# Attention rows set by a tile's number of keys, and eight rows of gathers alone, in a streaming encoder with gathered experts

## The chip, the core and the metric

The kernel runs on one core of a Trainium2 chip. The metric is the device time of one execution in microseconds (us), lower being better; a version is judged by the median of its runs.

## The reference

One layer of an encoder over 1024 prompt tokens and 128 sample tokens (eight requests of 16), each a vector of 1024 float32 values. What matters of it, shortened:

```python
a = rmsnorm(h)
qd, kd, vd, qs, ks, vs = split(a @ w_in)              # 8 heads of 64 each
w = softmax(qd1 @ kd1) - lam * softmax(qd2 @ kd2)     # differential attention, chunk-causal
diff = rmsnorm(w @ vd)
z = qs @ ks / 8                                       # stick-breaking attention, causal
wts = exp(log_sigmoid(z) + sum_of_later(log_sigmoid(-z)))
h += concat(diff, wts @ vs) @ w_out
# experts: per token 8 heads x 16 chosen of 16384
c = rmsnorm(h)
q = (c @ w_query).reshape(t, 8, 2, 128)
s1, i1 = top_k(q[:, :, 0] @ sub_keys[0].T, 16); s2, i2 = top_k(q[:, :, 1] @ sub_keys[1].T, 16)
top, sel = top_k(s1[..., None] + s2[..., None, :], 16)
idx = expert numbers of sel;  g = softmax(top)
coef = g * gelu(einsum('td,thkd->thk', c, expert_u[idx]))
h += einsum('thk,thkd->td', coef, expert_v[idx])
h += (p @ w_ple) * sigmoid(rmsnorm(h) @ w_pgate)
y = rmsnorm(h)
```

## The kernel before

Tokens are worked in nine tiles of 128 (`T = 9`; eight of the prompt, `TP = 8`, and one of the samples). Every token picks 128 experts, so a tile has 128 **rows** (`ROWS`): row r of a tile gathers, for each of the 128 tokens, one vector of `expert_u` and one of `expert_v`, 128 x 1024 floats each. There are 1152 rows in all, and the program is laid out along them. A **position** e is the 128 rows of tile e.

For one row: POOL issues the gather of u into a ring of four buffers (`gather_u`, L585) and, 16 rows later, the gather of v into a ring of eight (`gather_v`, L602). DVE takes the dot product of the u row with the tile's tokens (`dot`, L1498). After 16 rows ACT applies gelu (L1146) and DVE makes the coefficients (L1527). Of the v rows DVE adds some, those that the table `vector_rows` names (in the first 64 rows of a position four of 16, and five of 16 in positions 5 and 6), to `acc` (`add_row`, L1512). For the rest ACT spreads the coefficient onto a diagonal (`spread`, L1158, a ring of four) and PE multiplies with it into `sum_ps` (`add_rows`, L779). A gather waits until its buffer has been used: u on the dot four rows back, v on the sum eight rows back.

While the rows of tile e go through, the engines prepare tile e + 1, in two stages. **Attention** has four steps m = 0 to 3 (`attending_step`), each of two differential and two stick-breaking heads. In a step PE makes six score tiles in turn in two halves of `z_ps` (`attention_scores`, L810 and L812, j = 0 to 5). DVE takes the maximum of the first four (`maximum`, L1658), and ACT exponentiates each once its maximum is there (`softmax_top`, L1241). PE may overwrite a half only when that is done. Then come DVE's `subtract_half` (L1664 to L1669), ACT's `log_term` (L1249 to L1251), DVE's `break_stick` (L1677 to L1684), ACT's `raise_stick` (L1271), the transposes of the weights on PE (`turn_weights`, L825) with ACT's copies (L1258), and the products with the values (`weigh_values`, L837). For tile e + 1 a score tile has 128 x (e + 2) columns. **Routing** follows: `square_heads` and `norm_heads` on DVE with a power on POOL between them (`power`, L576), `turn_heads`, `project_heads` on PE (L722), `square_tokens` (L1559), then the queries, the key scores and the search for the best 16 on DVE, up to the new list of experts (L1645) and the gates.

The order of each engine is written out by hand. `go(end)` issues an engine's part of the rows up to `end`, and what follows it in the code stands behind those rows in that engine's queue. All engines are in order, so an operation that waits holds the rows behind it. Where things stand is given by two functions, `attend_at(e, m, k)` and `route_at(e, k)`: k counts 16 places in a step and 64 in the routing. In positions 1 to 6 the steps take rows 0 to 63 and the routing rows 64 to 127. Position 0 packs the four steps into rows 92 to 107 (the input projection runs before, L676), position 7 has the samples' attention in rows 0 to 79, and position 8 the end of the network (L1918 on). Before row 0 there are steps and a routing with no gathers beside them (e = -1). SP loads keys and values for a step when the former step no longer needs them (`load_keys`, `load_values`).

## Time and profile before

| | us |
|---|---|
| three runs | 4246.7, 4250.4, 4270.1 |
| median | 4250.4 |
| the profiled execution, its own time | 4267.0 |
| its span, first to last instruction | 4265.2 |
| PE busy | 3316.2 (78%) |
| DVE busy | 2908.0 (68%) |
| POOL busy | 2747.3 (64%) |
| ACT busy | 1164.7 (27%) |

The execution that was profiled is 16.6 us above the median of the three. Busy time of PE is modelled, since its matmuls overlap; the busy time of POOL is the issuing of gathers. An average over the span says little here, since positions have different limits: a position is read by the time between the dot of its first row and that of the next position's first row, and by what DVE and POOL wait for in it. Positions 1 to 6 lie between 881.6 and 3331.8 us of the span.

### The profile page before, as it was taken

The page shows a single profiled execution, that of the slowest core. Times are in us where ns is not written, and L with a number is a line of the kernel's source. Part 1 is how long each engine was busy: PE and PEld are TensorE (multiplying, and loading weights), DVE is VectorE, ACT ScalarE, POOL GpSimd, SP SyncE. Part 2 cuts the span into 40 slices and gives each one's busy share as a digit, 9 for nine tenths or more (in the row PEclk, how much of TensorE's full clock was granted, in tenths as well). Part 3 has the DMA queues.
Part 4 walks back from the last instruction along what each step waited for, and adds up shares of the span by engine and source line. Part 5 has one row for each costly group of instructions (what it writes and reads, how often), then busy time and mean ns, then how long its engine had stood idle before and what let it go on. Part 6 is the DMA issues. An engine that isn't in the chain of part 4 may idle for free.

```text
span 4265.2 us, 32462 instructions
## 1 busy us (share of the span) xinstructions
PE 3316.2 (78%) x9380; PEld 1593.9 (37%) x9380; DVE 2908.0 (68%) x5551; ACT 1164.7 (27%) x2256; POOL 2747.3 (64%) x2355
## 2 busy tenths in 40 slices
PE   7788976767968786887778778877887687758777
PEld 3334434333424433443344334433443343323333
DVE  2176754577687678768776877687768667686775
ACT  2211115134114312421342134313531233111111
POOL 0016653367777777777777776777677656567784
PEclk9899987988999999999899988999899998879998
DMA  5238987489999999999999999999999999899996
GB/s 197 92 135 319 344 335 248 157 302 372 342 354 380 370 329 358 379 345 357 350 324 335 340 343 334 330 351 353 340 335 366 338 327 357 313 336 370 378 373 234
DMA packets 452607, 1369.22 MB, mean 321 GB/s; under 512 B 47696, under 2 KB 118224, under 8 KB 451408
## 3 DMA queue, kind: packets, MB, share of 16 engines
q0 software_dynamic: 331776, 1208.11, 76.6%
q1 hardware_dynamic: 95312, 135.96, 9.2%
q10 hardware_dynamic: 25344, 23.07, 1.6%
q8 instruction: 79, 1.29, 0.1%
q14 instruction: 96, 0.79, 0.1%
HBM read 1338.65 MB, written 28.31 MB: 320 GB/s over the span
## 4 chain that ended last, share of the span: by engine, by line
PE 39%; POOL 21%; issue 13%; DVE 11%; DMA 10%; ACT 5%; another core or an unknown queue 1%; ACTq 0%; SPq 0%; POOLq 0%; DVEq 0%
PE sum_ps L779 14%; POOL v_ring L602 10%; POOL u_ring L585 10%; PE z_ps L722 7%; PE z_ps L676 6%; DMA u_ring<-expert_u_in,idx_tile 4%; DMA v_ring<-expert_v_in,idx_tile 4%; DVE u_ring L1498 3%; PE sum_ps L676 2%; PE z_ps L810 2%; DVE arena L1589 1%; PE out_ps L837 1%; DVE neg_max L1658 1%; PE z_ps L976 1%; PE group_ps L825 1%
## 5 line engine op out<-in xcount | busy, mean ns | idle before, releaser
L779 PE MATMUL sum_ps<-v_ring,diag 128*128 128x512 f32 x3172 | 1694.9, 671 | 631.8 <-DMA v_ring<-expert_v_in,idx_tile 342.9
L585 POOL DMA_INDIRECT u_ring<-expert_u_in,idx_tile x1152 | 1363.1, 1183 | 766.3 <-DVE dots L1498 417.3
L1498 DVE CUSTOM_DVE_ANT_0 u_ring<-u_ring,c_rows 128x1024 f32<-128x1024 f32 x1152 | 1404.6, 1225 | 598.3 <-DMA u_ring<-expert_u_in,idx_tile 535.4
L602 POOL DMA_INDIRECT v_ring<-expert_v_in,idx_tile x1152 | 1331.2, 1156 | 360.2 <-issue 327.9
L779 PEld LDWEIGHTS sum_ps<-v_ring,diag 128*128 128x128 f32 x3172 | 618.4, 210 | 1443.4 <-issue 894.7
L1512 DVE SCALAR_TENSOR_TENSOR acc<-v_ring,coef,acc 128x1024 f32<-128x1024 f32 x350 | 450.4, 1287 | 9.0 <-DMA v_ring<-expert_v_in,idx_tile 9.0
L1158 ACT ACTIVATE diag<-ident,coef 128x128 f32<-128x128 f32 x793 | 287.2, 394 | 517.1 <-PE sum_ps L779 369.2
L722 PE MATMUL z_ps<-weights,arena 128*128 128x512 f32 x768 | 343.2, 600 | 3.4 <-ACT arena L1120 3.4
L1658 DVE TENSOR_REDUCE neg_max<-z_ps 128x1 f32<-128x128 f32 (+7 forms) x128 | 96.5, 755 | 262.3 <-PE z_ps L812 231.7
L676 PE MATMUL z_ps<-weights,arena 128*128 128x512 f32 x576 | 257.9, 604 | 21.1 <-issue 12.3
L722 PEld LDWEIGHTS z_ps<-weights,arena 128*128 128x128 f32 x768 | 146.8, 193 | 182.9 <-issue 176.1
L1241 ACT ACTIVATE arena<-z_ps,neg_max 128x128 f32<-128x128 f32 (+7 forms) x128 | 94.7, 740 | 437.9 <-DVE neg_max L1658 347.8
L837 PEld LDWEIGHTS out_ps<-arena 128*128 128x128 f32 x1152 | 163.4, 210 | 103.1 <-issue 87.4
L810 PE MATMUL z_ps<-arena,qd 128*128 128x512 f32 (+3 forms) x384 | 149.6, 499 | 46.7 <-DMA qd<-qk_turned 40.6
L837 PE MATMUL out_ps<-arena 128*128 128x64 f32 x1152 | 158.2, 287 | 32.4 <-ACT arena L1258 25.7
L825 PE MATMUL group_ps<-ident,arena 128*128 128x128 f32 x576 | 104.2, 292 | 98.9 <-ACT arena L1258 86.6
L676 PEld LDWEIGHTS z_ps<-weights,arena 128*128 128x128 f32 x576 | 109.3, 193 | 155.7 <-issue 143.4
L676 PE MATMUL sum_ps<-weights,v_ring 128*128 128x512 f32 x288 | 141.7, 648 | 15.0 <-ACT v_ring L1187 6.3
L1258 ACT COPY arena<-group_ps 128x512 f32<-128x512 f32 (+3 forms) x192 | 90.6, 472 | 193.0 <-PE group_ps L825 147.1
L1146 ACT ACTIVATE gelus<-dots 128x16 f32<-128x16 f32 x72 | 15.4, 214 | 443.7 <-DVE dots L1498 294.6
L1589 DVE FIND_INDEX8 arena<-arena 128x8 uint32<-128x128 f32 (+1 forms) x432 | 134.4, 329 | 0.0
L608 POOL TENSOR_TENSOR p_stat<-p_stat,minus_half 128x1 f32<-128x1 f32 x9 | 9.6, 1061 | 193.2 <-DVE p_stat L1734 193.2
(189 smaller groups left out, 3106.4 us busy)
## 6 DMA issues: line engine op xcount, KB each, us to landing
u_ring<-expert_u_in,idx_tile POOLq DMA_INDIRECT x1152
v_ring<-expert_v_in,idx_tile POOLq DMA_INDIRECT x1152
weights<-w_in_in SPq DMA_DIRECT2D x6, 2048.0 KB, 18.6
u_ring<-w_query_in SPq DMA_DIRECT2D x16, 512.0 KB, 5.2
weights<-w_out_in SPq DMA_DIRECT2D x2, 4096.0 KB
weights<-w_query_in SPq DMA_DIRECT2D x1, 8192.0 KB, 39.4
qk_turned<-arena ACTq DMA_DIRECT2D x24, 256.0 KB, 4.5
arena<-x_all_in SPq DMA_DIRECT2D x9, 512.0 KB
```

Source lines behind the costliest of these rows:

```text
L585: pool.indirect_dma_start(u_rows[r % U_RING][:, :], None, ins["expert_u"], bass.IndirectOffsetOnAxis(ap=idx_tile[:, e % 2, at:at + 1], axis=0)
L602: pool.indirect_dma_start(v_rows[g % V_RING][:, :], None, ins["expert_v"], bass.IndirectOffsetOnAxis(ap=idx_tile[:, e % 2, at:at + 1], axis=0)
L676: mm = nc.tensor.matmul(bank, home.aT[:, k, :], w_in[:, k, g * W:(g + 1) * W], start=(k == 0), stop=(k == KC - 1))
L722: mm = nc.tensor.matmul(acc_ps[:, bank, :], inT[:, k, :], weights[:, k, half * W:(half + 1) * W], start=(k == 0), stop=(k == KC - 1))
L779: mm = nc.tensor.matmul(sum_ps[:, half * W:(half + 1) * W], diag[:, by_tensor[g] % DIAGS, :], v_rows[g % V_RING][:, half * W:(half + 1) * ...
L810: nc.tensor.matmul(z_ps[:, j % 2, a:a + w], q, kt.rearrange("p j k -> p (j k)")[:, a:a + w], start=True, stop=a + w < width)
L825: mm = nc.tensor.transpose(group_ps[:, (k - a) * P:(k - a + 1) * P], src[:, k * P:(k + 1) * P], const.ident)
L837: mm = nc.tensor.matmul(out_ps[:, 64 * h:64 * h + 64], wT[:, k * P:(k + 1) * P], v[:, k, 64 * (h % 2):64 * (h % 2) + 64], start=(k == 0), ...
L1158: nc.scalar.mul(diag[:, j % DIAGS, :], const.ident, coef[:, (step - 1) % 2, g % TOP:g % TOP + 1]).then_inc(diag_done, 1)
L1498: nc.vector.tensor_tensor_reduce(row, row, c_rows[e % 2][:, :], 1.0, 0.0, ALU.mult, ALU.add, dots[:, s % 2, r % TOP:r % TOP + 1]).then_inc ...
L1512: nc.vector.scalar_tensor_tensor(acc[:, :], row, weight, acc[:, :], ALU.mult, ALU.add).then_inc(v_added, 1)
L1589: last = nc.vector.max_index(found[:, m, 8 * half:8 * half + 8], vals[:, m, 8 * half:8 * half + 8], src[:, m, :])
```

## The change

Positions 1 to 6 get another table of rows. Rows 0 to 7 have neither attention nor routing (`LATER = 8`). The four steps then share 5e + 32 rows: 37 in position 1, 42, 47, 52, 57, and 62 in position 6, so that a step has 9.25 rows in position 1 and 15.5 in position 6, where it had 16 in each. The routing has what is left: 83 rows in position 1, then 78, 73, 68, 63, and 58 in position 6, where it had 64. Positions -1, 0, 7 and 8 keep their tables.

Beside this, some operations get another place k. On ACT each `softmax_top` now stands at the k of the maximum that it waits for (2, 3, 5, 6) instead of in pairs at 0 and 4. PE's scores j = 4 move from 4 to 5. In the routing `square_heads` moves from 2 to 4, `norm_heads` and PE's `turn_heads` from 4 to 5, `project_heads` 0 from 5 to 6, and POOL's first power from behind the gather of row 2 + 3 to behind that of 4 + 2. These moves hold in all positions.

```diff
+LATER = 8
+        def attention_rows(e):
+            return 5 * e + 32
         def attend_at(e, m, k):
-            return FREE_ROWS + 4 * m + k // 4 if e == 0 else ROWS * e + TOP * m + k
+            if e < 0:
+                return ROWS * e + TOP * m + k
+            if e == 0:
+                return FREE_ROWS + 4 * m + k // 4
+            return ROWS * e + LATER + (TOP * m + k) * attention_rows(e) // 64
         def route_at(e, k):
...
-            return ROWS * e + 64 + k
+            if e < 0:
+                return ROWS * e + 64 + k
+            return ROWS * e + LATER + attention_rows(e) + (ROWS - LATER - attention_rows(e)) * k // 64
...
-                go(route_at(e, 2) + U_RING)
+                go(route_at(e, 4) + U_RING - 1)
                 power(e + 1, 0)
...
-                go(attend_at(e, m, 4))
+                go(attend_at(e, m, 5))
                 attention_scores(i, 4, n)
...
-                go(attend_at(e, m, 0))
+                go(attend_at(e, m, 2))
                 softmax_top(i, 0, m, n)
+                go(attend_at(e, m, 3))
                 softmax_top(i, 1, m, n)
                 go(attend_at(e, m, 4))
                 if m:
                     take_out(e, m - 1)
+                go(attend_at(e, m, 5))
                 softmax_top(i, 2, m, n)
+                go(attend_at(e, m, 6))
                 softmax_top(i, 3, m, n)
...
-                go(route_at(e, 2))
+                go(route_at(e, 4))
                 square_heads(t)
-                go(route_at(e, 4))
+                go(route_at(e, 5))
                 norm_heads(t)
```

PE's `turn_heads` goes from `route_at(e, 4)` to `route_at(e, 5)` and `project_heads(t, 0)` from 5 to 6 in the same way.

**ACT, position 4, second step (m = 1), from its first exponential to the first `log_term`.** `diag` is the spread coefficient of a v row, `neg_max` the maximum that DVE makes. Before:

```order
L1241 ACT_TABLE_LOAD
L1241 ACTIVATE arena,total<-z_ps,neg_max 128x768 x2
L1158 ACTIVATE diag<-ident,coef 128x128 x4
L1265 COPY mix<-out_ps 128x2x128
L1241 ACTIVATE arena,total<-z_ps,neg_max 128x768 x2
L1158 ACTIVATE diag<-ident,coef 128x128 x3
L1249 ACTIVATE arena<-z_ps 128x768
```

After:

```order
L1252 ACTIVATE arena,total<-z_ps,neg_max 128x768
L1169 ACTIVATE diag<-ident,coef 128x128
L1252 ACTIVATE arena,total<-z_ps,neg_max 128x768
L1276 COPY mix<-out_ps 128x2x128
L1169 ACTIVATE diag<-ident,coef 128x128
L1252 ACTIVATE arena,total<-z_ps,neg_max 128x768 x2
L1260 ACTIVATE arena<-z_ps 128x768
```

Seven spread rows stood between the first exponential and the logarithm, and none between the first two exponentials; now two stand there, one of them between the first two.

**DVE, the same step, from its first maximum to the first `subtract_half`.** Before:

```order
L1658 TENSOR_REDUCE neg_max<-z_ps 128x1
L1498 ISA u_ring,dots<-u_ring,c_rows 128x1024
L1498 ISA dots 128x1
L1658 TENSOR_REDUCE neg_max<-z_ps 128x1
L1498 ISA u_ring,dots<-u_ring,c_rows 128x1024
L1498 ISA dots 128x1
L1498 ISA u_ring,dots<-u_ring,c_rows 128x1024
L1498 ISA dots 128x1
L1658 TENSOR_REDUCE neg_max<-z_ps 128x1
L1498 ISA u_ring,dots<-u_ring,c_rows 128x1024
L1498 ISA dots 128x1
L1658 TENSOR_REDUCE neg_max<-z_ps 128x1
```

After:

```order
L1672 TENSOR_REDUCE neg_max<-z_ps 128x1
L1512 ISA u_ring,dots<-u_ring,c_rows 128x1024
L1512 ISA dots 128x1
L1672 TENSOR_REDUCE neg_max<-z_ps 128x1
L1512 ISA u_ring,dots<-u_ring,c_rows 128x1024
L1512 ISA dots 128x1
L1512 ISA u_ring,dots<-u_ring,c_rows 128x1024
L1512 ISA dots 128x1
L1523 TENSOR_SCALAR acc<-v_ring,coef 128x1024
L1672 TENSOR_REDUCE neg_max<-z_ps 128x1 x2
```

The dot that stood between the third and the fourth maximum is gone from there; of the 16 rows of the step 13 are left.

## Rows read from the trace of the kernel before

**Rows 1.** From the page: the share of the DMA engines in 40 slices, in tenths.

```profile
DMA  5238987489999999999999999999999999899996
```

**Rows 2.** Windows: length; PE, PEld, DVE, ACT, POOL busy; clock; DMA share; GB/s.

```profile
881.60:1070.80 189.20, 137.30 (x410) 71.93 (x411) 132.32 (x214) 78.62 (x156) 146.46 (x129) 0.86 0.99 375
1070.80:1272.20 201.40, 162.55 (x392) 69.44 (x391) 149.45 (x362) 33.38 (x79) 154.98 (x132) 0.94 0.94 347
1272.20:1461.80 189.60, 147.11 (x462) 76.47 (x460) 139.13 (x214) 84.46 (x155) 145.41 (x128) 0.90 0.99 373
1461.80:1664.00 202.20, 162.08 (x395) 69.10 (x394) 149.31 (x362) 34.26 (x80) 152.42 (x133) 0.94 0.94 347
1664.00:1858.40 194.40, 154.79 (x568) 85.68 (x567) 147.00 (x215) 95.50 (x174) 152.96 (x127) 0.94 0.99 369
1858.40:2060.80 202.40, 159.40 (x387) 68.11 (x386) 149.25 (x361) 32.98 (x77) 156.15 (x133) 0.95 0.95 347
2060.80:2276.40 215.60, 169.53 (x611) 95.64 (x611) 154.13 (x214) 101.64 (x173) 155.68 (x125) 0.89 0.93 335
2276.40:2487.30 210.90, 164.46 (x394) 70.32 (x394) 149.09 (x362) 33.38 (x78) 156.37 (x133) 0.93 0.92 336
2487.30:2709.50 222.20, 179.96 (x636) 103.08 (x635) 166.03 (x217) 106.73 (x168) 157.29 (x128) 0.88 0.92 330
2709.50:2910.20 200.70, 157.37 (x400) 68.35 (x399) 149.24 (x362) 34.07 (x79) 154.42 (x133) 0.97 0.96 352
2910.20:3129.60 219.40, 182.12 (x667) 102.43 (x666) 172.78 (x218) 111.69 (x166) 153.03 (x127) 0.90 0.94 341
3129.60:3331.80 202.20, 162.10 (x423) 70.98 (x423) 151.16 (x368) 34.47 (x82) 154.66 (x130) 0.97 0.98 359
```

**Rows 3.** Waits in position 4's attention, 2060.8 to 2276.4: total, times, longest.

```profile
ACT arena L1241 <- DVE neg_max L1658: 63.6, 14, 9.2
...
DVE neg_max L1658 <- PE z_ps L812: 28.7, 6, 7.5
...
POOL u_ring L585 <- DVE dots L1498: 24.6, 9, 5.2
```

**Rows 4.** Waits in position 1's attention, 881.6 to 1070.8.

```profile
DVE u_ring L1498 <- DMA u_ring<-expert_u_in,idx_tile: 45.3, 38, 3.0
PE sum_ps L779 <- ACT diag L1158: 34.0, 7, 20.6
```

**Rows 5.** Timeline of one step's start in position 4: start, us, what, idle before.

```profile
2181.64 6.57 PE L779 MATMUL sum_ps<-v_ring,diag 128*128 128x512 f32 x8 [6.44 <-issue]
...
2189.76 0.96 DVE L1658 TENSOR_REDUCE neg_max<-z_ps 128x1 f32<-128x768 f32 x1 [6.09 <-PE z_ps L812]
...
2192.12 0.94 POOL L585 DMA_INDIRECT u_ring<-expert_u_in,idx_tile  x1 [5.06 <-DVE dots L1498]
...
2194.30 3.60 PE L779 MATMUL sum_ps<-v_ring,diag 128*128 128x512 f32 x8
```

**Rows 6.** Windows of position 0's four steps, four rows and 256 keys each.

```profile
660.80:683.20 22.40, 14.79 (x53) 10.58 (x53) 15.73 (x29) 14.75 (x28) 10.70 (x8) 0.67 0.65 208
683.20:703.50 20.30, 16.22 (x65) 10.14 (x64) 11.30 (x25) 13.35 (x29) 7.62 (x8) 0.92 0.70 234
703.50:724.80 21.30, 17.45 (x67) 10.97 (x66) 11.26 (x25) 13.32 (x29) 7.63 (x8) 0.84 0.72 237
724.80:744.00 19.20, 15.27 (x60) 9.34 (x58) 11.19 (x24) 13.49 (x30) 7.61 (x8) 0.91 0.64 203
```

**Rows 7.** Lines by shape, position 4's attention: count, busy, mean ns, idle before.

```profile
L1498 DVE CUSTOM_DVE_ANT_0 u_ring<-u_ring,c_rows 128x1024 f32<-128x1024 f32 x64 | 77.4, 1222 | 26.8 <-DMA u_ring<-expert_u_in,idx_tile 26.2 <-issue 0.4
...
L1512 DVE SCALAR_TENSOR_TENSOR acc<-v_ring,coef,acc 128x1024 f32<-128x1024 f32 x16 | 20.7, 1294 | 0.0
```

**Rows 8.** Waits in the first 32 routing rows of position 1, 1070.8 to 1174.3.

```profile
DVE mix L1559 <- PE z_ps L722: 5.8, 1, 5.8
...
POOL rstat L576 <- DVE rstat L1564: 5.1, 1, 5.1
```

More of the change, by code:

```diff
@@ L1013, in _ @@
                 t = e + 1
-                go(route_at(e, 4))
+                go(route_at(e, 5))
                 turn_heads(t)
-                go(route_at(e, 5))
+                go(route_at(e, 6))
                 project_heads(t, 0)
@@ L1855, in _ @@
                 go(route_at(e, 1))
-                go(route_at(e, 2))
+                go(route_at(e, 4))
                 square_heads(t)
-                go(route_at(e, 4))
+                go(route_at(e, 5))
                 norm_heads(t)
```

## The prediction

> **What bounds the kernel now.** I first read the share of the DMA engines along the span [rows 1]: it stands at nine tenths in almost every slice from the tenth on. So for most of the time the gathers themselves are the bound, and a change of order can only win what is missing to a full share. The page's slices are too coarse to say where that is, so I cut positions 1 to 6 into their attention and routing halves of 64 rows [rows 2]; the two halves of a position are two neighbouring rows there. Three things are to be seen. In positions 1 to 3 the attention halves take 189.2, 189.6 and 194.4 us at a share of 0.99: 2.96 us a row, and nothing to win. In positions 4 to 6 they take 215.6, 222.2 and 219.4 us at 0.92 to 0.94. The routing halves take 200.7 to 210.9 us at 0.92 to 0.98. Multiplying each length by what its share lacks of one gives 2 + 12 + 2 + 12 + 2 + 12 + 15 + 17 + 18 + 8 + 13 + 4 = 117 us. That is about all that this change can gain.
>
> Then I asked who makes the late attention halves slow. In position 4 POOL stands still for 24.6 us before u gathers, in nine waits, until a dot has freed a buffer, and DVE stands for 28.7 us in six waits for PE's score tiles; ACT waits 63.6 us for maxima [rows 3]. The timeline of one step links them [rows 5]. ACT has taken up its first pair of exponentials, which wait for DVE's maxima two and three rows further on, so it spreads no coefficients, and PE is idle for 6.44 us. When it goes on, its eight matmuls of v rows take 6.57 us, where eight of the same kind take 3.60 us a little later. Only behind them come the scores for the third maximum. DVE waits 6.09 us for these, no dot is done, and POOL waits 5.06 us. The ring of four u buffers is then used up and the DMA engines run out of work. In position 1 the same ACT block exists (PE waits 34.0 us for the diagonals), but PE has little to do there, and DVE's own idle time is nearly all for u rows, 45.3 us [rows 4]; so it costs nothing.
>
> **The price of a row and of a step.** The profiled execution took 4267.0 us, 16.6 us more than the median of 4250.4 us; I work out a difference in the former and take it off the latter. A row that nothing else delays costs 2.95 us, from position 1's attention (189.2 / 64 [rows 2]); I use it for rows alone too. On DVE one row costs 1.22 us for the dot (77.4 / 64) and 1.29 us for each added v row, 16 of them in 64 rows [rows 7], so 1.54 us. For positions 5 and 6 I count 5 in 16, as the table of added rows has it, so 1.62 us.
>
> A step costs the larger of two things: its rows at 2.95 us, or DVE's own work plus w, the time that DVE waits in it for its partners. DVE's work per step is the busy time of the attention half less the rows that leave it, over four: position 1 (132.3 - 27 x 1.54) / 4 = 22.7 us, then 26.3, 30.2, 33.9, position 5 (166.0 - 7 x 1.62) / 4 = 38.7, and 42.4 us [rows 2]. The rows at 2.95 us are 27.3, 31.0, 34.7, 38.4, 42.0 and 45.7 us. So the new table puts the steps close to DVE's own work everywhere, and w decides.
>
> **What w will be.** No row shows it for the new steps. From below: in position 1's attention DVE is idle for 189.2 - 132.3 = 56.9 us, 45.3 of them for u rows [rows 2, 4], which leaves 2.9 us a step at 16 rows. From above: position 0 packs a step of 256 keys into four rows, and DVE is idle there for 6.7, 9.0, 10.0 and 8.0 us, 8.4 us on average [rows 6], with nearly no rows to fill the waits. By row count between these two, steps of 9 to 12 rows have about 5.5 us: I take that for positions 1 to 3. In position 4 it is now (215.6 - 154.1 - 26.2) / 4 = 8.8 us [rows 2, 7], and the block described above is most of it. With each exponential at the place of its maximum, ACT can spread before it and PE is not starved before the third score tile. But the first maximum of a step now comes one row after the scores were asked for instead of two, and the third and fourth stand together. I take 7 us for positions 4 to 6, between 5.5 and 8.8.
>
> **Attention, the sum.** Eight rows alone are 23.6 us, and four steps follow. Position 1: 23.6 + 4 x 28.2 = 136.4, against 45 rows now at 2.96 = 133.0: +3. Position 2: 150.8 against 50 rows, 148.1: +3. Position 3: 23.6 + 4 x 35.7 = 166.4 against 167.1: -1. Position 4: 23.6 + 4 x 40.9 = 187.2 against 60 rows at 3.37, 202.1: -15. Position 5: 206.4 against 222.2 and one routing row, 225.3: -19. Position 6: 23.6 + 4 x 49.4 = 221.2 against 219.4 and six routing rows, 238.4: -17. Together -46 us. With w = 2.9 everywhere all steps fall to their rows' price and the sum is -96; with w = 8.4 everywhere it is +6.
>
> **Routing, the sum.** The routing half of position 1 is 201.4 - 64 x 2.95 = 12.6 us over its rows. Its first 32 rows take 1174.3 - 1070.8 = 103.5 us, 9.1 over 32 x 2.95, and in them DVE waits 5.8 us for PE's product before `square_tokens`, and POOL 5.1 us for the second power [rows 8]. The distance from `norm_heads` to `square_tokens` was 6 rows (k 4 to 10) and is 6 again in position 1 (row 51 to 57), so I keep the 9.1 us; in positions 4 to 6 it is 5 rows. What goes with 83 rows is the crowding of the searches, 3 or 4 us. So position 1: 83 x 2.95 + 9.1 = 254.0 against 19 attention rows and 201.4, 257.6: -4. In the same way positions 2 and 3 give -4 and -5, position 4 (68 rows, its surplus kept) -2, position 5 (63 rows) 0, position 6 (58 rows, surplus of 13.4 us in fewer rows) +3. Together -12 us; between 0, if all the surplus is in fixed waits, and -30, if half of it goes.
>
> **The smaller edits.** POOL's first power now stands one gather earlier while the squares stand where they did relative to it or later, so POOL holds u row 4 + 3 until a dot, the squares and the power are done. Free at best, and at worst once the 5.1 us of a power's wait [rows 8] in each of six positions; I take +1 us each, +6, since three u rows are in flight then. Position 7's squares come two rows later, which gives the samples' rows more time to land; position 0's, one row. I cost these at nothing: neither is at a place where DVE is ahead. The keys of a step are reloaded once its fourth score tile is read, and have 7 rows of time in position 1 where they had 13; at 2.95 us that is 21 us, for 192 KB at 375 GB/s. It stays hidden.
>
> **The forecast:** -46 - 12 + 6 = -52 us. 4267.0 becomes 4215, and the median 4250 becomes **4198 us**.
>
> **Rivals.** First, **the DMA engines fill up**: w falls to what position 1 shows, and the routing loses half its surplus. The sum is -96 - 30 + 6 = -120, capped by the 117 us above: 4133 us. For it speaks that positions 1 to 3 hold 0.99 in attention; against it, that DVE's work in the late steps is within 4 us of the rows' price.
>
> Second, **the gain is given back in the early positions**. They have 0.99 now and can only lose. If a step of 9 to 12 rows waits as long as one of four, w = 8.4 us, positions 1 to 3 lose 15 + 14 + 11 us, and 4 to 6 gain only 9 + 13 + 12: +6 - 12 + 6 = 0, so 4250 us. For it: the wait for a step's own chain (scores, maximum, exponential, logarithm, scan, exponential, transpose, product) does not shrink with the rows. Against it: those waits are hidden by dots and added rows, of which there are twice as many or more.
>
> Third, **slower, by PE's clock**. The granted clock is 0.86 to 0.90 in five attention halves of six [rows 2], that is a part of the time at the lower of its two levels, and the two groups of eight matmuls, 6.57 us after an idle stretch of 6.44 us and 3.60 us in full work [rows 5], show the two levels, 1.2 and 2.4 GHz. The change adds eight rows of little PE work before each attention, and in the routing of positions 1 to 4 spreads the work thinner. If each step starts at the lower level, its scores, and again its last transposes and products, take twice as long on the path of w. I put that at 5 us a step, from the 3 us by which the slow group exceeds the fast one, once at the start and less at the end. Over 24 steps it is +120, so +68 in all: 4318 us. It decides from 3 us a step on. Against it: ACT's block, which now makes PE idle, goes. The Trainium skill, in "TensorE: Matmul & The Clock Gate", Part 1 on the clock gate, says that the throttled state is the default and that activity releases it, which speaks for this rival; by that rule alone sparse rows before each attention bring the time to this rival's 4318 us, and by the granted clock of 0.94 to 0.97 in the routing halves, themselves sparse in PE work, to none of it.
>
> That the change does nothing is no rival: the orders differ in every step.
>
> **How the numbers follow.** The forecast has 0.50, the first rival 0.12, the second 0.21, the third 0.17. What a measurement of this kernel can tell from no change is about 0.5%, 21 us. Faster by more than that are the first rival and nearly all of the forecast's spread, and a little of the second: 0.64. Within it: 0.19. Slower: 0.17. The range takes in w from 2.9 us, -96 - 12 + 6 = -102, 4148 us and somewhat below, and above the second rival with 25 us of the way to the third: 4140 to 4275 us. The forecast's own range is 4160 to 4232 us.
>
> **What would show it.** In the profile of the changed kernel: the DMA share of positions 4 to 6 up to 0.95 or more over their attention rows, with POOL's wait for dots there down from 24.6 us to some 12; ACT's wait for maxima halved and PE's wait for diagonals in position 1 well under 34.0 us; position 1 as long as now within 5 us and positions 5 and 6 shorter by 15 to 20 us each. If w is wrong, the early positions show it: at 8.4 us position 1 is over 10 us longer and its attention share under 0.95. If the clock is the cause, the granted clock of the attention rows falls below 0.8. It would also be wrong if the eight rows alone cost more than 2.95 us each, or if the routing's surplus grew in positions 5 and 6 by more than the 3 us counted.

## The result, and the profile after

| | before | after |
|---|---|---|
| runs, us | 4246.7, 4250.4, 4251.1, 4270.1 | 4309.0, 4319.9, 4324.7, 4328.4 |
| median | 4250.7 | 4322.3 |
| ratio, 95% interval | | 1.0124 [1.0087, 1.0161] |
| profiled execution, and its span | 4267.0, 4265.2 | 4328.4, 4326.6 |
| positions 1 to 6 in it | 2450.2 | 2504.8 |

The changed kernel is slower, where I had forecast 4198 us: by 1.2% by the ratio on record, by 1.7% by the two medians. Why the two differ is not shown. A ratio of 1.0124 belongs to a kernel before of 4269 us, and beside the first experiments below it did run at 4268.8 us. The fourth run of the kernel before, 4251.1 us, is new here. In the profiled executions positions 1 to 6 lose 54.6 us, position 7 loses 9, position 8 loses 3, and position 0 gains 6.

The page of the changed kernel looks almost like the one of before: the busy times of the engines, and the share of the DMA engines in tenths, to be held against [rows 1].

```profile
PE 3371.6 (78%) x9380; PEld 1616.6 (37%) x9380; DVE 2905.5 (67%) x5551; ACT 1159.6 (27%) x2249; POOL 2731.4 (63%) x2355
...
DMA  5348997489999999999999999899899889899996
```

Only five eights in the slices 26 to 35, where there was one, tell that something was lost. Cut into stages it is plain. These are windows of the changed kernel (length; PE, PEld, DVE, ACT, POOL busy; granted clock; DMA share; GB/s): the four steps of positions 1 and 2, which answer to the attention rows in [rows 2] but hold 37 and 42 rows and not 64, and the four steps of positions 3, 4 and 6 with 47, 52 and 62 rows.

```profile
900.40:1020.10 119.70, 95.47 (x330) 54.38 (x329) 89.91 (x152) 65.60 (x126) 84.53 (x74) 0.87 0.94 353
1299.40:1438.60 139.20, 111.55 (x401) 62.12 (x399) 104.52 (x163) 78.91 (x137) 97.78 (x83) 0.90 0.93 344
1700.90:1868.50 167.60, 138.34 (x486) 80.36 (x485) 119.26 (x174) 85.98 (x150) 112.64 (x93) 0.83 0.91 326
2119.20:2304.50 185.30, 151.22 (x553) 88.02 (x553) 135.40 (x187) 95.68 (x159) 130.13 (x103) 0.89 0.91 323
2964.90:3185.50 220.60, 178.76 (x673) 102.17 (x672) 169.18 (x211) 109.64 (x164) 154.48 (x122) 0.91 0.90 326
```

Before, the share was 0.99 in positions 1 to 3 and 0.92 to 0.94 in the later ones [rows 2]. Now it is 0.90 to 0.94 in all of them: the early positions have lost their full share, and the late ones have gained none to speak of. A row of the steps costs 3.24 us in position 1 (119.7 / 37) and 3.57 us in position 3. By stage, in us (first dot to first dot, one profiled execution):

| position | 8 rows alone | four steps | routing | sum | before |
|---|---|---|---|---|---|
| 1 | 24.1 | 119.7 | 258.3 | 402.1 | 390.6 |
| 2 | 21.0 | 139.2 | 241.9 | 402.1 | 391.8 |
| 3 | 20.3 | 167.6 | 230.0 | 418.0 | 396.8 |
| 4 | 20.6 | 185.3 | 214.7 | 420.7 | 426.5 |
| 5 | 20.6 | 197.0 | 206.8 | 424.3 | 422.9 |
| 6 | 21.4 | 220.6 | 195.5 | 437.5 | 421.6 |

Next, who waits. These are waits of the changed kernel in position 4's steps, in the form of [rows 3] (waiter and line, what it waits for; total, times, longest in us; L1252 is the exponential, L1672 the maximum, L596 the gather of u, L1512 the dot; `remote` is a release that the profile ties to no instruction).

```profile
ACT arena L1252 <- DVE neg_max L1672: 47.4, 12, 23.7
...
POOL u_ring L596 <- DVE dots L1512: 26.8, 9, 6.4
...
DVE neg_max L1672 <- PE z_ps L823: 24.3, 5, 9.9
...
DVE neg_max L1672 <- remote: 8.3, 1, 8.3
```

POOL still waits 26.8 us for dots, and DVE some 33 us for score tiles, now in fewer and longer waits. The place has changed. I added up DVE's idle time before each maximum of a step, over the 24 steps of positions 1 to 6: before the third maximum it was about 96 us and is now 3, as forecast; before the fourth it was 4 and is now 14; but before the **first** it was about 41 us and is now 132. A timeline (start, us, what, idle before) of the start of position 3's third step shows what a first maximum waits for.

```profile
1793.75 1.33 PE L848 MATMUL out_ps<-arena 128*128 128x64 f32 x10 [0.35 <-ACT arena L1269]
...
1794.92 1.30 PE L821 MATMUL z_ps<-arena,qd 128*128 128x512 f32 x4
...
1796.05 0.39 PE L823 MATMUL z_ps<-chunk_mask,ident 128*128 128x128 f32 x2
...
1796.48 0.82 DVE L1672 TENSOR_REDUCE neg_max<-z_ps 128x1 f32<-128x640 f32 x1 [7.11 <-PE z_ps L823]
...
1798.71 0.95 POOL L596 DMA_INDIRECT u_ring<-expert_u_in,idx_tile  x1 [3.47 <-DVE dots L1512]
```

The scores of a new step stand on PE behind the products with the values of the step before, and these wait for ACT's copies of the transposed weights. That tail (scan, exponential, transposes, copies, products) takes its time whatever the number of rows. With 16 rows in a step it was mostly over when DVE came to the first maximum; with the 11 or 12 here it is not: DVE stands for 7.11 us, and POOL for 3.47 us after it.

Two more waits are to be seen in position 6's steps. L1523 is DVE's first addition of a position, which overwrites `acc` and so needs the former tile's output to be stored; L1541 makes the coefficients after a gelu.

```profile
POOL u_ring L596 <- DVE dots L1512: 29.9, 6, 12.0
...
DVE acc L1523 <- DMA summed<-acc: 13.3, 1, 13.3
...
DVE coef L1541 <- ACT gelus L1157: 11.4, 2, 6.4
```

### The profile page after: what moved, and what is told of

Its sections match the earlier page's. It is cut to its first block, busy times and chain, and to the rows that moved or that the text cites. A ratio compares the mean times of both kernels' runs of the same rounds, so it can differ in the third digit from the quotient of the medians.

```text
span 4326.6 us, 32452 instructions
## 1 busy us (share of the span) xinstructions
PE 3371.6 (78%) x9380; PEld 1616.6 (37%) x9380; DVE 2905.5 (67%) x5551; ACT 1159.6 (27%) x2249; POOL 2731.4 (63%) x2355
## 3 DMA queue, kind: packets, MB, share of 16 engines
q0 software_dynamic: 331776, 1208.11, 75.6%
## 4 chain that ended last, share of the span: by engine, by line
PE 27%; POOL 18%; issue 13%; DVE 12%; DMA 9%; ACT 6%; another core or an unknown queue 1%; SPq 0%; ACTq 0%; DVEq 0%; POOLq 0%
PE sum_ps L790 12%; POOL u_ring L596 9%; POOL v_ring L613 9%; PE z_ps L733 6%; DMA v_ring<-expert_v_in,idx_tile 4%; DMA u_ring<-expert_u_in,idx_tile 4%; DVE u_ring L1512 3%; PE z_ps L821 2%; PE out_ps L848 2%; DVE arena L1603 2%; PE group_ps L836 1%; DVE acc L1526 1%; ACT arena L1269 1%; PE z_ps L687 1%
## 5 line engine op out<-in xcount | busy, mean ns | idle before, releaser
L790 PE MATMUL sum_ps<-v_ring,diag 128*128 128x512 f32 x3172 | 1716.8, 679 | 564.2 <-DMA v_ring<-expert_v_in,idx_tile 344.8
L596 POOL DMA_INDIRECT u_ring<-expert_u_in,idx_tile x1152 | 1341.3, 1164 | 840.4 <-DVE dots L1512 498.9
L1512 DVE CUSTOM_DVE_ANT_0 u_ring<-u_ring,c_rows 128x1024 f32<-128x1024 f32 x1152 | 1402.5, 1225 | 582.0 <-DMA u_ring<-expert_u_in,idx_tile 506.9
L790 PEld LDWEIGHTS sum_ps<-v_ring,diag 128*128 128x128 f32 x3172 | 628.6, 213 | 1404.5 <-issue 843.1
L1672 DVE TENSOR_REDUCE neg_max<-z_ps 128x1 f32<-128x128 f32 (+7 forms) x128 | 96.1, 755 | 272.1 <-PE z_ps L823 238.1
L1252 ACT ACTIVATE arena<-z_ps,neg_max 128x128 f32<-128x128 f32 (+7 forms) x128 | 94.6, 740 | 370.4 <-DVE neg_max L1672 310.0
L836 PEld LDWEIGHTS group_ps<-ident,arena 128*128 128x128 f32 x576 | 75.8, 159 | 160.9 <-ACT arena L1269 119.4
```

Of the source, the lines that this page charges most:

```text
L596: pool.indirect_dma_start(u_rows[r % U_RING][:, :], None, ins["expert_u"], bass.IndirectOffsetOnAxis(ap=idx_tile[:, e % 2, at:at + 1], axis=0)
L790: mm = nc.tensor.matmul(sum_ps[:, half * W:(half + 1) * W], diag[:, by_tensor[g] % DIAGS, :], v_rows[g % V_RING][:, half * W:(half + 1) * ...
L836: mm = nc.tensor.transpose(group_ps[:, (k - a) * P:(k - a + 1) * P], src[:, k * P:(k + 1) * P], const.ident)
L1512: nc.vector.tensor_tensor_reduce(row, row, c_rows[e % 2][:, :], 1.0, 0.0, ALU.mult, ALU.add, dots[:, s % 2, r % TOP:r % TOP + 1]).then_inc ...
```

## The experiments

Ten kernels ran, in three groups. Each group had the kernel before beside it on its own chip, where its median was 4268.8, 4278.2 and 4298.9 us, so ratios to it are compared, not times. The first group has the two orders alone, the eight rows alone and the store first on the changed kernel; the third has the two kernels with later maxima; the second has the rest. None of them leaves out work. Stage times are from one profiled execution each, of positions 1 to 6. The runs of one kernel lie 9 to 45 us apart, so a difference of a few us between two kernels' stages means nothing by itself.

### The order of attention alone

```diff
-                go(attend_at(e, m, 0))
+                go(attend_at(e, m, 2))
                 softmax_top(i, 0, m, n)
+                go(attend_at(e, m, 3))
                 softmax_top(i, 1, m, n)
...
-                go(attend_at(e, m, 4))
+                go(attend_at(e, m, 5))
                 attention_scores(i, 4, n)
```

with exponentials 2 and 3 at 5 and 6, on the table of before.

> The kernel before with one part of the change alone: the exponentials of ACT at the places of their maxima and PE's fifth score tile one place later; all tables of rows as before. Theory (the loss comes from the denser steps, the order itself helps): DVE's wait for the third maximum, 4 to 7.5 us in each step of positions 4 to 6, goes, and the time falls by 30 to 45 us, to 4206 to 4220 us. Rival (the order moves the wait to the next step's first maximum): 4250 us within 10, with first waits of 7 us or more. Rival (the order is what makes the changed kernel slow): over 4270 us.

Measured: 4221.9 us, ratio 0.9895 [0.9875, 0.9915], some 45 us, as expected. This is the fastest of all, and faster than both kernels of the case. Its positions 1 to 6 take 2399.6 us, 50.6 less than before. Windows of its attention, 64 rows each, in positions 1, 4, 5 and 6:

```profile
876.70:1064.90 188.20, 139.83 (x394) 72.49 (x395) 131.85 (x215) 77.58 (x151) 143.89 (x130) 0.83 1.00 382
2061.60:2259.30 197.70, 163.73 (x612) 92.60 (x611) 155.06 (x215) 103.64 (x174) 157.63 (x127) 0.95 0.99 367
2463.00:2662.50 199.50, 171.02 (x641) 99.55 (x640) 166.59 (x218) 109.41 (x170) 159.12 (x126) 0.91 0.98 367
2865.60:3068.80 203.20, 174.63 (x668) 99.64 (x667) 173.22 (x217) 113.48 (x167) 150.92 (x126) 0.94 0.99 365
```

The late ones took 215.6, 222.2 and 219.4 us at 0.92 to 0.94 [rows 2]; they are now at 0.98 and 0.99. And its waits in position 4, against [rows 3]:

```profile
ACT arena L1241 <- DVE neg_max L1661: 26.5, 11, 5.7
...
DVE neg_max L1661 <- PE z_ps L812: 1.8, 2, 1.1
...
POOL u_ring L585 <- DVE dots L1501: 1.7, 1, 1.7
```

ACT's wait for maxima fell from 63.6 to 26.5 us, DVE's for scores from 28.7 to 1.8, and POOL's for dots from 24.6 to 1.7. So the part of the change that puts an exponential at the place of its maximum is worth 1% by itself, and what is left of the change, the table of rows, costs 2.3% beside it (1.0124 over 0.9895 is 1.023; with the two medians of the case it would be 2.8%), if the two add up.

### The order of routing alone

`square_heads` at 4, `norm_heads` and `turn_heads` at 5, `project_heads` 0 at 6, and POOL's first power one gather earlier, all as in the change, on the table and the attention order of before.

> The kernel before with the moves of the routing alone (squares and norm of the heads, the turn, the first projection, POOL's first power). Theory: within 8 us of before, 4243 to 4259 us. Rival (these moves hold POOL's gathers back in every position, 5 us each): 4280 us.

Measured: 4271.6 us, 1.001 [0.9991, 1.0029]; positions 1 to 6 take 2445.0 us against 2450.2. These moves do nothing that can be measured, and the rival's 5 us in every position is excluded. The 6 us in all that I had put on the power lie inside the interval, so they are neither shown nor refuted.

### Eight rows alone, but 64 rows of attention

```diff
         def attention_rows(e):
-            return 5 * e + 32
+            return 64
```

on the changed kernel. Steps have 16 rows again; the routing is left with 56.

> The changed kernel with 64 rows of attention in each of positions 1 to 6, behind the eight rows alone; the routing has 56 rows. Theory (the density of the steps is the cause): the first maximum of a step waits under 3 us in positions 1 to 3, these are each 10 to 15 us shorter than in the changed kernel in their attention, and the time is 4235 to 4265 us, with some 20 us lost in the routing by 56 rows. Rival (the eight rows and the sum's change in the middle of a step are the cause): the second step is still the slow one, 55 us or more, and the time stays at 4300 us or above.

Measured: 4366.4 us, 1.0221 [1.0193, 1.0249]; positions 1 to 6 take 2550.5 us. That thin steps are the only cause is refuted: with full steps the kernel got slower still, though in part by a wait that was small in the changed kernel. Its second step of a position takes 53 to 66 us. Asked what DVE's first addition (L1523, nine times) waits for, its trace answers:

```profile
L1523 DVE TENSOR_SCALAR acc<-v_ring,coef x9: 746/752/754, 336.6 to 3991.0; 128x1024 f32<-128x1024 f32 x9
...
  DMA summed<-acc: 90.3, 6
```

15 us in each of six positions. SP stores the tile's output behind the values of the second step, which it loads only when the former step's products have read the old ones. With the table moved by eight rows this comes later than the addition that needs the store. I had walked past this queue in the prediction.

### The store ahead of the values

```diff
                 for m in range(4):
                     load_keys(i, m)
-                    load_values(i, m)
                     if i >= 2 and m == 1:
                         store(i - 2)
+                    load_values(i, m)
```

Done once on the changed kernel:

> The changed kernel with SP's store of the finished sum ahead of the values of the second step instead of behind them. Theory: DVE's wait of 13.3 us for the store in position 6 and of 1.8 us in position 5 goes, and the time falls by 8 to 15 us, to 4307 to 4314 us. Rival (the wait is only taken over by the next one of the same step): 4322 us within 5.

Measured: 4306.8 us, 1.0078 [1.0053, 1.0103], and no wait for the store is left, where the changed kernel had 15.1 us in two waits. Positions 1 to 6 take 2490.1 us, 14.7 less than the changed kernel. The two intervals overlap, though, and of the 14.7 us position 3, which had no such wait, has 11.3 and position 6 has 6.7: that the store costs this much in the changed kernel is likely, not shown. And once on the kernel with 64 rows behind eight:

> The run e4 (eight rows alone, then steps of 16 rows) with SP's store of the finished sum ahead of the values of the second step. Theory (DVE waits 13 to 15 us in each of the six positions for that store, and most of it is lost time): 55 to 80 us below e4, 4286 to 4311 us, with rows 24 to 39 of a position at 52 us or less. Rival (the wait is cover for others): within 20 us of e4, 4345 us or above.

Measured: 4324.8 us, 1.0118 [1.0074, 1.0161]: a gain of 1.0% on the run above, some 44 us where 55 to 80 were expected, with intervals that don't overlap; positions 1 to 6 take 2509.1 us. Windows of position 4, steps and routing:

```profile
2121.90:2332.70 210.80, 164.00 (x610) 93.65 (x608) 154.38 (x214) 98.34 (x168) 157.37 (x126) 0.91 0.94 343
...
2332.70:2523.30 190.60, 151.46 (x368) 66.88 (x369) 137.01 (x342) 31.01 (x73) 138.02 (x117) 0.92 0.91 328
```

By the ratios the store is 0.5% of the change's loss. Without it the two tables, thin steps with long routing and full steps with short routing, are 0.4% apart, which the intervals don't separate, and both are some 2% behind the order of before with its exponentials moved. So with full steps, and without the late store, eight rows alone in front still cost 2.2% (1.0118 over 0.9895), about as much as the whole table of the change.

Two things make up this cost, read against the kernel with the attention order alone. The eight rows take only 20 to 24 us, 2.7 us a row, but the 56 rows of routing behind them still take 191.9 us on average, where 64 took 204.5: a row taken out of the routing gives back 1.6 us, not 2.95. And the steps, 16 rows each in both kernels, take 1230.0 us in the six positions against 1172.3, so 57.7 us more (in position 4, 210.8 against 197.7). Nothing was made thinner there; the steps only stand elsewhere among the rows. DVE's idle time before it makes coefficients is 50.9 us in these steps and was 3.7. The coefficients of 16 rows fall due where a step used to begin, and that is now its middle. Position 4's main wait of this kind:

```profile
DVE coef L1541 <- ACT gelus L1157: 9.0, 3, 5.5
```

### Fewer rows for attention, none alone

The best kernel so far, the one with the attention order alone, with another split in two sizes (it has the changed kernel's functions for the places):

```diff
+LATER = 0
+        def attention_rows(e):
+            return 56
```

> The run e1 (the kernel before with the attention's order alone) with attention in rows 0 to 55 of positions 1 to 6, 14 rows a step, and routing in 72 rows; no rows alone. Theory (a step is bound by its own chain, so a row taken out of it saves about 1.7 us and costs 2.95 us or more in the routing): 20 to 50 us above e1, 4242 to 4272 us, most of it in positions 4 to 6. Rival (density costs nothing, the shift does): within 10 us of e1, 4212 to 4232 us.

Measured: 4259.8 us, 0.9962 [0.9935, 0.999], which is 0.7% over the kernel with 64 rows. Its steps are 88 us shorter in the six positions for 48 rows fewer, 1.8 us a row, and its routing is 134 us longer for 48 rows more, 2.8 us a row. Position 4, steps and routing:

```profile
2069.00:2250.50 181.50, 149.66 (x578) 87.31 (x577) 142.00 (x197) 99.38 (x164) 143.61 (x111) 0.94 0.97 353
...
2250.50:2481.30 230.80, 176.45 (x425) 74.27 (x424) 161.28 (x379) 36.29 (x86) 172.33 (x150) 0.93 0.93 343
```

Then `return 48`, with `LATER = 2`, 12 rows a step:

> As e8, with two rows alone and then 12 rows a step, attention in rows 2 to 49. Theory: waits of 6 to 10 us for the first maximum of the steps in positions 4 to 6, a step there no shorter than 45 us, position 1 unchanged within 6 us; 80 to 170 us above e1, 4300 to 4390 us. Rival (density costs nothing): 4240 us or less.

Measured: 4318.2 us, 1.0126 [1.0059, 1.0193], 2.3% over the 64 rows and as slow as the changed kernel. Its steps in positions 1, 4 and 6:

```profile
891.60:1032.50 140.90, 114.23 (x379) 61.75 (x377) 106.87 (x178) 72.59 (x141) 109.21 (x97) 0.90 1.01 381
...
2083.90:2256.90 173.00, 140.42 (x552) 83.24 (x551) 129.21 (x178) 92.99 (x154) 125.23 (x95) 0.94 0.91 323
...
2938.10:3136.70 198.60, 163.34 (x628) 96.86 (x627) 147.55 (x178) 105.59 (x152) 122.15 (x96) 0.89 0.84 299
```

48 rows at 3.60 us in position 4 and at 4.14 us in position 6, where 64 rows cost 3.09 and 3.18 us each. Thin steps lose, and the more so the fewer rows they have, as expected; DVE's idle time before first maxima goes from 29 us with 64 rows to 94 with 56 and 165 with 48. Here no step is shifted by eight rows, and the store is not late; with 56 rows DVE has no idle time before coefficients in the steps either, so there the loss is the thinning alone (with 48 rows that idle time is 17.6 us). Two expectations for 48 rows were missed: five of the twelve steps in positions 4 to 6 took 38 to 42 us where none under 45 was expected, and position 1 is 6.9 us shorter than with 64 rows, not unchanged within 6.

### Sixteen rows alone

With eight rows alone the coefficients of 16 rows fall due in the middle of a step, and DVE waits for ACT's gelu there; with 16 they would again fall due at its start. So `LATER = 16`, 64 rows of attention, 48 of routing, the store first, and the routing order of before.

> The run e1 with the steps shifted by 16 rows, attention in rows 16 to 79 and routing in 48, the store of the sum first as in e7. The steps stand to the groups of 16 rows as in the kernel before, but the sum changes inside the first. Theory (a shift by half a group puts gelu and the coefficients into the middle of a step's chain): the four steps take 3 to 10 us less per position than in e7, and DVE's waits for gelu under 1 us each. The routing in 48 rows takes 180 us or more against 203 us for 64 rows in e1, so the total is 4350 to 4420 us. Rival (the routing's time goes with its rows): 4260 us or less.

Measured: 4420.7 us, 1.0325 [1.0274, 1.0375]. DVE's waits for gelus fell from 51 us to 4 in the attention rows, but the four steps came out at 214.5 us a position and not below the 205.0 of the eight-row kernel: the store is late again (it still stands behind the keys of the second step), 75.6 us before L1523 in six waits, and the first steps are 56 to 72 us long. Without their first step they are 2.9 us shorter. The expectation was missed, and how much the moved gelus cost by themselves stays open. The routing behind shows again what squeezing it brings; position 4:

```profile
2424.80:2602.00 177.20, 138.53 (x340) 61.97 (x339) 125.16 (x324) 26.80 (x63) 117.33 (x101) 0.90 0.85 305
```

177.2 us for 48 rows, at a share of 0.85. On average it is 177.7 us, somewhat under the 180 expected, and again 1.7 us back for each row taken out of 64. I read this as a chain that the stage has of its own; no run here takes that chain apart.

### Later maxima

If a first maximum only stands too early in a short step, it should help to move it. Scores 2 to 5 on PE, the four maxima on DVE and the four exponentials on ACT go to places 4 to 7, and the first subtraction, logarithm and transposes to 8. On the changed kernel with its store first:

```diff
-                go(attend_at(e, m, 2))
+                go(attend_at(e, m, 4))
                 maximum(i, 0, n)
-                go(attend_at(e, m, 3))
+                go(attend_at(e, m, 5))
                 maximum(i, 1, n)
```

> The run e6 (the changed kernel, store of the sum first) with the four maxima of a step, their exponentials and the score tiles behind them at places 4 to 7 instead of 2, 3, 5 and 6, and the first subtraction at 8, so that three or four rows stand ahead of a step's first maximum instead of one or two. Theory (a dense step is bound by the length of its chain, and where DVE waits in it does not matter): the wait for the first maximum falls by half or more, later waits grow, and the time is within 0.4% of e6, 1.004 to 1.012 of before. Rival (the loss is the place of the first maximum, one row behind the scores): 0.6% or more below e6, at or under 1.002 of before.

Measured: 4378.7 us, 1.0197 [1.0151, 1.0243], 1.2% over the same kernel without the move. On the best kernel, with 16 rows a step:

> The same move of the maxima on the run e1, with 16 rows a step. Theory: e1 waits 52 us in all for maxima in positions 1 to 6, 26 of them for first ones; with three rows ahead these go, and the time is 0 to 15 us below e1, 0.986 to 0.9895 of before. Rival (the chain behind the maxima then has too few rows, and the wait moves there): 0.992 or above.

Measured: 4286.9 us, 0.9971 [0.9948, 0.9994], 0.8% slower than it. The group of all maxima on the page (x128; busy, mean ns; idle before them and its main releaser), first of the changed kernel, then of the one with later maxima:

```profile
L1672 DVE TENSOR_REDUCE neg_max<-z_ps 128x1 f32<-128x128 f32 (+7 forms) x128 | 96.1, 755 | 272.1 <-PE z_ps L823 238.1
```

```profile
L1671 DVE TENSOR_REDUCE neg_max<-z_ps 128x1 f32<-128x128 f32 (+7 forms) x128 | 96.7, 757 | 290.8 <-PE z_ps L823 216.8
```

and of the kernel with the attention order alone:

```profile
L1661 DVE TENSOR_REDUCE neg_max<-z_ps 128x1 f32<-128x128 f32 (+7 forms) x128 | 96.3, 754 | 172.0 <-PE z_ps L812 153.8
```

Putting the maxima later doesn't take the wait away, 290.8 against 272.1 us (275.8 with the store first); it moves it. Over the 24 steps of positions 1 to 6, and against the same kernel without the move, the wait before first maxima fell from 134 to 75 us and the one before third maxima rose from 5 to 59. I read this as the chain of a step starting later and so ending later. The sum of these waits grew by 7 us only, while positions 1 to 6 took 45.1 us more (with 16 rows a step, 38.0 us more), so most of the loss is not in them. Some 17 us of each may be the third group's chip, where the kernel before is 0.7% slower. And part of both ratios lies outside these steps: in position 0, where a step has four rows and the move reaches it too, the four steps of the kernel with 16 rows took 144.0 us instead of 84.0, and the whole position 606.7 us instead of 580.8. What is refuted is that a later first maximum helps; what remains is the length of the chain against the length of the step.

## Why the prediction was wrong, point by point

**Where the loss is.** Positions 1 to 6 of the profiled executions, each line from the positions' sums, with us a position in the last column:

| from, to | us | where it lies |
|---|---|---|
| before, attention order alone | -50.6 | -8.4: ACT's block ahead of the third maximum |
| attention order, changed kernel with store first | +90.5 | +15.1: rows alone +21.1; steps -25.8 for 14.5 rows fewer; routing +19.7 for 6.5 rows more |
| store first, changed kernel | +14.7 | +2.4: in part DVE behind the late store, 15.1 us in two waits |
| sum | +54.6 | 2450.2 to 2504.8 |

In the second line a row taken out of the steps gives back 1.8 us, and one put into the routing costs 3.0 us. Rows alone are cheap, 2.6 us, but the eight that stand there were taken out of the steps at 1.8. These are differences of single executions.

**The bound and the first diagnosis** were right. ACT's early exponentials held PE, PE the third score tile, and that the u ring; undoing only this won 50.6 us in positions 1 to 6 of the 117 us that the shares lacked. I had put -46 us on the whole of attention; the order of attention alone, without the table, brings -58 us in the attention rows.

**The term that failed is w, DVE's wait in a step.** The forecast took 5.5 us in positions 1 to 3 and 7 us in 4 to 6. Worked out from the trace after by the same formula (a step's mean length less DVE's work per step) it is 7.2, 8.5, 11.7, 12.4, 10.5 and 12.8 us, 10.5 on average. The step that failed is the choice of bounds: I read w at 16 rows from position 1 and at four rows from position 0, found 2.9 and 8.4, and took these for the ends. Both are of short tiles, with 384 and 256 keys. The chain of a step grows with the keys, to 1024 in position 6, and its tail reaches into the next step, so 8.4 us was no upper bound. The kernel with 48 rows shows the growth at one row count: with 12 rows in each step DVE is idle for 8.5, 8.2, 11.4, 11.0, 11.1 and 12.8 us a step in positions 1 to 6.

The trace of before had a warning. The prediction worked w out for position 4 alone, 8.8 us. By the same sum position 5 has (222.2 - 166.0 - 15.0) / 4 = 10.3 us, over the supposed upper end at 16 rows a step. Its 15.0 us are the wait for u rows:

```profile
DVE u_ring L1498 <- DMA u_ring<-expert_u_in,idx_tile: 15.0, 11, 3.1
```

Two limits of this reading. The 2.9 and 8.8 us leave out the wait for u rows, and the 10.5 holds it; without it the changed kernel's w is 5.8, 7.5, 11.7, 11.2, 7.5 and 10.0 us, 9.0 on average, so in position 1 the forecast was good and in position 5 nearly. And w isn't the chain alone: steps of 16 rows became 2.4 us longer by standing behind eight rows (57.7 us over 24 steps). In the changed kernel DVE's idle time before coefficients is 25.6 us, 1.1 us a step, of the 4.3 by which the term was too small.

By the prediction's sums each further us of w costs 24 us, one in each step. Attention came out at +43 us against -46, and (10.5 - 6.25) x 24 = 102 us, less the 14 us by which the rows alone were cheaper, is 88 of these 89. That it closes is no proof, since w was worked out from the same lengths; it says that no other term of attention failed.

**The other terms.** The rows alone were priced at 2.95 us and cost 2.67 on average (128.0 us for 48 of them), which is 14 us less. Routing was put at -12 and POOL's power at +6; by the same comparison (against the same number of rows of before) it came out at +11: +1, -2, 0, -10, +9, +12. The forecast saw position 6 at +3; a surplus in fixed waits, which does not shrink with the rows, is the mechanism named, and its size was wrong. The power's +6 can't be told from nothing by the run of the routing order alone. The late store, 13.3 us in position 6 and 1.8 in position 5, was not in the sum at all: the note on SP went over the keys, which SP does reload in time, and not over the store behind the values.

**The signs that were named.** Position 1 over 10 us longer with a share under 0.95 was the sign of a wrong w: it is 11.5 us longer, at 0.94. PE's wait for diagonals in position 1 fell from 34.0 [rows 4] to 9.1 us, and DVE's for u rows from 45.3 to 6.7 (in 37 rows instead of 64), since DVE is now late itself:

```profile
PE sum_ps L790 <- ACT diag L1169: 9.1, 5, 3.3
...
DVE u_ring L1512 <- DMA u_ring<-expert_u_in,idx_tile: 6.7, 7, 1.6
...
DVE neg_max L1672 <- PE z_ps L823: 10.8, 6, 5.4
```

ACT's wait for maxima in position 4 was to halve from 63.6 us and is 47.4. POOL's wait for dots was to fall from 24.6 to 12 and is 26.8. The share in positions 4 to 6 was to reach 0.95 and is 0.90 to 0.93.

**The rivals.** The second, gain given back in the early positions by a wait that does not shrink with the rows, is the mechanism that ran, with the shift of the coefficients beside it; what spoke against it (twice as many dots and sums to hide the waits) was too little, and its w of 8.4 us was too small, so it stopped at no change. The third, PE's clock, gave 4318 us, nearly the time measured; that is chance, for it is not the main cause. Its sign, a granted clock under 0.8, is absent: the six attention stages have 0.87, 0.90, 0.83, 0.89, 0.92 and 0.91, against 0.86, 0.90, 0.94, 0.89, 0.88 and 0.90 before. In position 3 a part of it is real. The products with the values there, grouped by line, the changed kernel's behind that of before:

```profile
L837 PE MATMUL out_ps<-arena 128*128 128x64 f32 x150 | 18.9, 275 | 0.0
```

```profile
L848 PE MATMUL out_ps<-arena 128*128 128x64 f32 x140 | 22.6, 323 | 1.4 <-ACT arena L1269 1.1 <-issue 0.4
```

That is 140 x 48 ns = 7 us more, and with scores, masks and transposes 13 us in this position. The same difference over all six is 1, 4, 13, 5, -4 and 3 us, 22 us in sum and 0.9 us a step, where the rival needed 3 to decide and had 5. Over the whole execution PE is busy for 55.4 us more with the same matmuls (3371.6 against 3316.2), at a mean granted clock of 0.900 against 0.914, and how much of that lies on the path is not shown. But the loss of thin steps comes without it: the kernel with 56 rows is 0.7% slower than the one with 64 with PE busy for 3.0 us more (3330.3 against 3327.3). The Trainium skill, in "TensorE: Matmul & The Clock Gate", Part 1, says that the throttled state is the default and activity releases it. By that the sparse rows ahead of the steps would lower the clock. The trace agrees in part: it has 0.76 for the eight rows alone of position 1, 0.92, 0.92 and 0.94 for those of positions 2 to 4, and 0.83 and 0.84 for those of 5 and 6, but the steps behind them have no lower clock than before except in position 3.

**Open.** Each of the two is shown by itself, thin steps without a shift (0.7% and 2.3%) and a shift with full steps (57.7 us in them), but how the changed kernel's loss divides between its chain and the gelus that fall due in its middle wasn't settled, since the kernel with 16 rows alone brought the store back. The table of rows with the old attention order wasn't tried either, so that the two parts of the change add up is argued from the runs around it.

## What to carry to other kernels

In engines that work in order, put an operation that waits at the place of what it waits for; this alone was worth 1%. Before rows are moved from one stage to another, ask of each stage what a row gives back when it leaves: a stage whose own chain is about as long as its rows gives back less (here 1.6 to 1.8 us) than the row costs elsewhere (2.7 to 3.0 us in the routing), and the bound for that chain must come from a stage with the same data, not from a shorter one. When a table of places shifts, follow every queue through it, those of stores and loads too, and ask which regular work of the rows, here the coefficients of every 16, now falls into the middle of a chain.

## What the runs showed of the hardware beside this

I had taken 0.99 of the DMA engines' share for a full load, and 2.95 us for the least that a row can cost. The rows alone of the changed kernel go faster; position 3, eight rows:

```profile
1680.50:1700.90 20.40, 13.14 (x25) 4.67 (x24) 12.37 (x20) 3.36 (x7) 15.52 (x17) 0.92 1.03 408
```

408 GB/s and 2.55 us a row, at a share of 1.03, against 375 GB/s at 0.99 in [rows 2]: 9% more bytes at 4% more share. So a share near one is no full load. In the attention rows the engines also load keys and values. The queues (packets, MB, share of the 16 engines) tell what those cost: first position 1's attention before (189.2 us; `software_dynamic` is the gathers, `hardware_dynamic` the loads), then the gathers of the window above (20.4 us).

```profile
q0 software_dynamic: 18541, 67.52, 93.9%
q1 hardware_dynamic: 4465, 3.28, 5.3%
```

```profile
q0 software_dynamic: 2280, 8.30, 102.2%
```

Per full share the gathers move 380 GB/s in the first and 398 in the second, and the loads 327. The loads are 5% of the bytes, so that their packets are slower accounts for less than one of the 9 per cent. The larger parts are the higher share and the gathers' own packets, which go 5% faster in the rows alone; why, no run here shows.
